# The input projection of a hybrid decoder layer by Strassen's scheme for pairs of token tiles, and a feed-forward pass in two groups

## What is computed

```python
hn = rmsnorm(x, norm1_g[l])
proj = hn @ w_in[l]                       # 1024 x 3608
q_a, k_a, v_a, gate_a, low_a, qkv_b, z_b, beta_b, dec_b = jnp.split(proj, IN_IDX, axis=-1)
...
o_a, h_a = gla_chunked(q, k, v, log_a.reshape(B, T, H_GLA, DK_GLA), st_gla[l])
...
o_b, h_b = gdn_chunked(qd, kd, vd, g, beta, st_gdn[l])
...
mix = jnp.concatenate([o_a.reshape(B, T, GLA_V), o_b.reshape(B, T, GDN_V)], axis=-1)
x = x + mix @ w_out[l]
hn2 = rmsnorm(x, norm2_g[l])
up, ffn_new = causal_dwconv(hn2 @ w_up[l], st_ffn[l], ffn_conv_w[l])
a_f, b_f = jnp.split(up, [D_FF], axis=-1)
x = x + (jax.nn.silu(a_f) * b_f) @ w_down[l]
```

## Time and profile before

| | us |
|---|---|
| median of 3 runs | 3298.98 |
| lowest and highest | 3298.91, 3301.03 |
| the profiled execution | 3301.26 |
| its span on the core | 3299.5 |
| TensorE busy in it | 3198.2 |
| VectorE | 2063.4 |
| ScalarE | 859.1 |
| GpSimd | 581.5 |

### The profile page before, as it was taken

One profiled execution on the slowest core, in us unless ns is written; L12 is line 12 of the kernel. 1 busy time (PEld: TensorE's weight loads), 2 busy tenths in 40 slices (PEclk: granted clock), 3 DMA queues, 4 the chain that ended last, 5 costly groups with the idle time before them and its releaser, 6 DMA issues.

```text
span 3299.5 us, 59597 instructions
## 1 busy us (share of the span) xinstructions
PE 3198.2 (97%) x23585; PEld 2178.1 (66%) x23585; DVE 2063.4 (63%) x4876; ACT 859.1 (26%) x1897; POOL 581.5 (18%) x945
## 2 busy tenths in 40 slices
PE   7999999999999999996799999999999999999999
PEld 3555555556555555554477777777768877888775
DVE  1566665655566665655566566666686666666668
ACT  1223333233223332232322111111232222222223
POOL 1111111111111111112231121111063112111110
PEclk9999999999999999997799999999999999999999
DMA  6022222222222212215531111111133111111112
GB/s 239 9 84 84 84 65 84 84 63 67 65 79 84 84 65 84 79 53 154 156 98 39 49 53 39 39 51 39 39 114 126 39 50 40 52 39 39 40 38 77
DMA packets 225314, 236.56 MB, mean 72 GB/s; under 512 B 14268, under 2 KB 169444, under 8 KB 225043
## 3 DMA queue, kind: packets, MB, share of 16 engines
q1 hardware_dynamic: 225043, 232.81, 22.4%
HBM read 203.10 MB, written 29.67 MB: 71 GB/s over the span
## 4 chain that ended last, share of the span: by engine, by line
PE 48%; DVE 1%; POOL 1%; ACT 0%; issue 0%; DVEq 0%; POOLq 0%
PE mlp_bank L2135 32%; PE mlp_bank L2209 15%; PE mlp_bank L2223 2%; DVE mcv L2577 0%; POOL acc L2457 0%; PE mlp_bank L2215 0%; POOL acc L2462 0%; DVE acc L2638 0%; ACT mcv L2298 0%; PE mlp_bank L2234 0%; PE mlp_bank L2221 0%; DVE raw L2521 0%; ACT mth L2312 0%; DVE mcv L2581 0%; ACT raw L2353 0%
## 5 line engine op out<-in xcount | busy, mean ns | idle before, releaser
L696 PE MATMUL mixer_bank<-arena,hnt 128*128 128x451 f32 x2048 | 868.0, 555 | 15.5 <-DMA arena<-in_w_in_dram 8.4
L2135 PE MATMUL mlp_bank<-arena,ws 128*128 128x176 f32 (+1 forms) x3520 | 657.6, 340 | 10.6 <-ACT raw L2325 9.0
L2135 PEld LDWEIGHTS mlp_bank<-arena,ws 128*128 128x128 f32 x3520 | 588.8, 190 | 49.0 <-ACT raw L2325 10.2
L696 PEld LDWEIGHTS mixer_bank<-arena,hnt 128*128 128x128 f32 x2048 | 367.4, 191 | 307.6 <-issue 302.6
L2209 PE MATMUL mlp_bank<-arena 128*128 128x512 f32 x1120 | 493.7, 592 | 0.0
L2610 DVE TENSOR_TENSOR acc<-acc,mlp_bank 128x512 f32<-128x512 f32 x560 | 370.5, 686 | 57.0 <-PE mlp_bank L2209 54.5
L2209 PEld LDWEIGHTS mlp_bank<-arena 128*128 128x128 f32 x1120 | 211.2, 190 | 231.7 <-issue 205.3
L2577 DVE SCALAR_TENSOR_TENSOR mcv<-raw,cf,mcv 128x512 f32<-128x512 f32 (+2 forms) x440 | 287.3, 670 | 68.5 <-ACT mcv L2298 58.2
L646 POOL TENSOR_TENSOR ex<-dtt,level 128x512 f32<-128x512 f32 (+1 forms) x114 | 142.9, 1253 | 939.8 <-DVE dtt L1645 641.6
L2135 PE MATMUL mlp_bank<-arena 128*128 128x176 f32 (+1 forms) x1320 | 254.9, 343 | 5.2 <-PEq L2720 4.3
L730 PE MATMUL mixer_bank<-wo,th 128*128 128x512 f32 x512 | 249.0, 609 | 3.0 <-DMA wo<-in_w_out_dram 2.4
(11 more groups left out here) (368 smaller groups left out, 3619.3 us busy)
## 6 DMA issues: line engine op xcount, KB each, us to landing
wo<-in_w_out_dram SPq DMA_DIRECT2D x260, 256.0 KB, 2.7
arena<-in_w_up_dram SPq DMA_DIRECT2D x44, 512.0 KB, 4.9
wu<-in_w_up_dram SPq DMA_DIRECT2D x44, 512.0 KB, 4.9
arena<-in_w_down_dram SPq DMA_DIRECT2D x40, 512.0 KB, 4.1
arena<-in_w_in_dram SPq DMA_DIRECT2D x7, 1804.0 KB, 16.2
...
```

Of the source, the lines that this page charges most:

```text
L696: x = pe.matmul(bank[ring(g)][0:N, 0:GW], hnt[:, k, 0:N], w[:, k, g * GW:(g + 1) * GW], start=(k == 0), stop=(k == KT - 1))
L2135: x = pe.matmul(out[:, 0:N], left[:, k, :], xb[:, slot, k, g * N:(g + 1) * N], start=first and k == 0, stop=k == HK - 1, skip_group_check= ...
```

## The change

**The projection.** Tiles 0 and 1 are both projected ahead of mixer 0, by 16 units (column group, tile) of eight matmuls in four banks. VectorE meanwhile forms sixteen sums T1 to T4 of weight halves (each 128x1804), in place of the arena's upper columns; SyncE stores them to DRAM (14.8 MB). The other fourteen tiles go in pairs: the mixers 2p and 2p+1 host the tiles 2p+2 and 2p+3. Each host computes seven products for each of two column groups, 14 products of four matmuls, 56 in place of 64. Their left operands (`xops`) are made once for a pair by eight GpSimd operations, `x_operands`; their right operands come partly from the arena and partly, ten chunks of 924 KB per host, through a ring of four buffers which SyncE fills. Eight products' results are copied out of their bank by ScalarE (`keep`), six are added to copies by VectorE (`make_c11`, `make_c12`, `make_c22`); SyncE stores the blocks to DRAM (12 per pair) and reloads `proj` whole (`load_proj`, 1.85 MB) ahead of each mixer.

**The slots.** The output projection stands in slots 0 to 4, 6, 8 and 10, the products in 28 others; 13, 19, 23 and 39 are empty. The banks of the y transposes change (7 in place of the projection's), and the second half of them waits for the copy of the first. ScalarE squares the tokens of a coming tile ahead of ked. The sample's projection is wholly in mixer 14, for which SyncE loads the upper half of w_in again (7.4 MB), and mixer 15 has none.

**Feed-forward.** The second pass takes two groups of 264 columns.

```diff
+HW = NIN // 2
+OUT_SLOTS = {0: 0, 1: 1, 2: 2, 3: 3, 4: 4, 6: 5, 8: 6, 10: 7}
+PRODUCT_SLOTS = {slot: p for p, slot in enumerate([5, 7, 9, 11, 12, 14, 15, 16, 17, 18, 20, 21, 22, 24] + list(range(25, 39)))}
...
+            def ring_chunk(n):
...
+                t, i = divmod(n, CHUNKS)
+                if n >= 4:
+                    before, k = divmod(n - 4, CHUNKS)
+                    sp.wait_ge(s_products, PRODUCTS * before + (k + 3 if k < 5 else k + 5))
...
+            def host(t):
...
+                load_proj(t + 1)
+                n = CHUNKS * t
+                even = t % 2 == 0
+                ring_chunk(n + 4)
+                if even:
...
+            sp.wait_ge(s_stage_stored, stored(HOSTS))
+            sp.wait_ge(s_products, PRODUCTS * HOSTS)
+            for g in range(4, GROUPS):
+                w_group(g)
             wo_chunks(t - 1, 20)
+            load_proj(t + 1)
...
+            def x_operands(p):
+
+                c, done = 2 * p + 2, 7 * p
...
+                if p:
+                    gp.wait_ge(s_products, PRODUCTS * 2 * p)
...
+                gp.tensor_tensor(a11, xc[:, 0:HK_IN, :], scale[0], ALU.mult).then_inc(s_xops_made, 1)
+                gp.tensor_tensor(hnt[:, 0:HK_IN, :], hnt[:, 0:HK_IN, :], scale[1], ALU.mult)
+                gp.tensor_tensor(a12, xc[:, HK_IN:KT, :], scale[0], ALU.mult).then_inc(s_xops_made, 1)
+                gp.tensor_tensor(a22, hnt[:, HK_IN:KT, :], scale[1], ALU.mult).then_inc(s_xops_made, 1)
+                gp.wait_ge(s_xops_made, done + 3)
+                gp.tensor_tensor(s1, hnt[:, 0:HK_IN, :], a22, ALU.add).then_inc(s_xops_made, 1)
+                gp.wait_ge(s_xops_made, done + 4)
+                gp.tensor_tensor(s2, s1, a11, ALU.subtract).then_inc(s_xops_made, 1)
+                gp.tensor_tensor(s3, a11, hnt[:, 0:HK_IN, :], ALU.subtract).then_inc(s_xops_made, 1)
+                gp.wait_ge(s_xops_made, done + 6)
+                gp.tensor_tensor(s4, a12, s2, ALU.subtract).then_inc(s_xops_made, 1)
+            x_operands(0)
             for t in range(1, TILES):
                 mixer(t, t + 1, False, True)
+                if t % 2 and t < HOSTS - 1:
+                    x_operands((t + 1) // 2)
...
+            def project_first(i, g, tile):
+
+                if i >= 4:
+                    pe.wait_ge(s_proj_out if FIRST[i - 4][1] == 0 else s_one_out,
+                               sum(e == FIRST[i - 4][1] for _, e in FIRST[:i - 3]))
+                if i < 2:
...
+                    x = pe.matmul(bank[(0, 1, 3, 4)[i % 4]][:, 0:GW], first_x[tile][:, k, :], weight(k, g),
                                   start=(k == 0), stop=(k == KT - 1))
...
+            def product(t, part):
+
+                q, half = divmod(part, 2)
+                pair = 7 * (t // 2)
+                j = column_group(t, q // 7)
+                run, add = bank[1], bank[0]
...
+                    n = CHUNKS * t + (q - 2 if q < 7 else q - 4)
+                    if half == 0:
+                        pe.wait_ge(s_ring_loaded[n % 4], 16 + 16 * (n // 4 + 1))
+                    right = wx[n % 4]
+                    left, out, first = {2: (S2_X, run, False), 3: (S1_X, add, True), 4: (S3_X, run, False),
+                                        5: (S4_X, add, False), 6: (A22, run, False), 9: (S1_X, add, True),
+                                        10: (S2_X, run, False), 11: (S4_X, add, False), 12: (S3_X, run, False),
+                                        13: (A22, run, False)}[q]
+                for k in range(2 * half, 2 * half + 2):
+                    x = pe.matmul(out[:, 0:GW], xops[:, left, k, :], right[:, k, :], start=first and k == 0,
+                                  stop=k == HK_IN - 1, skip_group_check=not first)
+                if half == 1:
+                    x.then_inc(s_products, 1)
...
+                    for slot in range(i, j):
+                        if slot in OUT_SLOTS:
+                            if t:
+                                project_out(t, OUT_SLOTS[slot], C, lambda: None)
+                        elif slot in PRODUCT_SLOTS:
+                            part = PRODUCT_SLOTS[slot]
+                            if t < HOSTS:
+                                product(t, part)
+                            elif t == HOSTS and part < KT:
+                                project_sample(0, part)
+                            elif t == HOSTS and part >= 12 and part % 2 == 0:
+                                project_sample(1, part // 2 - 6)
                 return fill
...
             def turn_y(t):
                 def turn(half):
 
-                    if t < TILES - 1:
-                        pe.wait_ge(s_proj_out, GROUPS * (t + 1) + 3 + half)
-                        y_turn(t, C, half)
-                    elif half == 1:
-                        pe.wait_ge(s_proj_out, GROUPS * (t + 1) + 8)
-                        y_turn(t, C, 0)
-                        y_turn(t, C, 1)
+                    if half == 0:
+                        pe.wait_ge(s_sg_new, t + 1)
+                    else:
+                        pe.wait_ge(s_hs_half, t)
+                    y_turn(t, C, half)
...
+            def keep(t, q, block, source):
+
+                act.wait_ge(s_products, PRODUCTS * t + q + 1)
...
+                    act.wait_ge(s_stage_stored, stored(t))
...
                     y_square(t, C)
+                    act.wait_ge(s_y_normed, 3 * t - 2)
+                front(0)
 
                 act.wait_ge(s_q_turned, n)
                 act.activation(qsq[0:N, :, :], heads(3)[0:N, :, :], ACT.Square).then_inc(s_q_squared, 1)
...
+            def add_product(t, q, out, block, bank_):
+
+                dve.wait_ge(s_products, PRODUCTS * t + q + 1)
+                v = stage[4 * (q // 7) + block]
+                if out is None:
+                    out = v
+                return dve.tensor_tensor(out, v, bank_[:, 0:GW], ALU.add)
+
...
+                    if a == 1 and hosts:
+                        make_c12(t, 0)
                     if a == 1 and out and not sample:
-                        if not last_prompt:
-                            keep_y_half(t, C, 0)
+                        keep_y_half(t, C, 0)
                     if a == NL - 1:
...
-        PASSES = ((0, 2, 256, 0, 8), (T // 2, 3, 176, 8, 9))
+        PASSES = ((0, 2, 256, 0, 8), (T // 2, 2, 264, 8, 9))
```

791 lines of the change are left out of this document (517 added, 274 removed).

## The result

| | median us | lowest, highest | runs |
|---|---|---|---|
| before | 3298.94 | 3297.58, 3301.03 | 4 |
| changed | 3433.94 | 3428.73, 3443.64 | 4 |

The ratio is 1.041, with a 95% interval of 1.0398 to 1.0423: 135 us slower, where +71 and at most 3410 were forecast. The profiled execution of the changed kernel took 3443.64 us (span 3441.9), the slowest of the four.

What follows compares the result with a forecast made beforehand. The prediction took chains over VectorE and ScalarE, not TensorE, to bound the mixers. Its terms, 38.9 + 4.4 + 27 + 5 + 1 + 9.4 - 9.6 - 1 - 4, summed to +71: 3370 us, range 3315 to 3410.

Steps and rivals of the forecast that it cites:

- TensorE is the bound: Rival: whatever matmul time TensorE is spared comes off, about 3250 us; chance 0.08.
- Term 1: Ahead of mixer 0: projecting tiles 0 and 1 up front starts mixer 0 at 109.5 instead of 70.64, +38.9 us.
- Term 2: Steady hosts 1 to 13: with four slots left empty, a mixer goes from 92.6 to 93.0 us, +4.4 together.
- Term 4: Clock: new waits, twice a mixer, may halve TensorE's granted clock; 0 to +44 us in 26 waits, taken as +5.
- rival with both costs near their upper bounds: GpSimd blocks VectorE for whole operations or the clock falls at each wait: 3390 to 3410 us; chance 0.18.
- Term 3: Head of mixers 2, 4, ... 12: GpSimd's operand operations delay ug and lengthen VectorE's; 4.5 us each, +27, between 0 and +50.
- Term 5: Other mixers: mixer 0 +1, mixer 14 +9.4 (waiting for w_out), mixer 15 -9.6, the sample's own mixer -1 us.
- Term 6: Feed-forward, second pass: two groups of 264 columns give -3 and fewer stalls -1, together -4 us.
- The starved queue: Rival: SyncE's one queue starves TensorE in every mixer, 5 us per host, 3435 us; chance 0.07.

Runs made afterwards that it cites:

- move_four: Changed kernel with product parts in other slots: 19, 23 and 39 filled, 13, 25, 36 and 37 empty; 3392.6 us.
- cover_39: Changed kernel with two unread 128x451 matmuls added in empty slot 39 of mixers 0 to 13; 3412.9 us.
- move_slots: Changed kernel with the same product parts in other slots: 19 and 39 filled, 25 and 36 empty in their place; 3386.7 us.
- ffn_only: Kernel before with only the feed-forward's second pass changed to two groups of 264 columns; 3294.7 us against 3301.3, ratio 0.9980.
- narrow_ops: move_slots with the eight GpSimd operand operations of mixers 2, 4, ... 12 cut to 2 of 128 columns; 3354.0 us.

## Why the prediction was right and wrong

**The bound: right.** Chains, not TensorE, limit a mixer. Taking 6.1 us of matmuls out of it gave no time back: mixer 5's 98.2 us less the 5.1 of the clock is 93.1, for 93.0 forecast, and the waits stand where the forecast put them, within 0.1 us. The rival "TensorE is the bound" is out, with every host at 94.9 us or more. The chain can be shorter than 93.0, though: emptying slots 25 and 36, where TensorE showed no hole, did give time, and move_four has odd mixers of 91.7 and 91.9 us at full clock throughout. The change left its empty slots where VectorE and ScalarE held TensorE anyway.

**Term 1: right.** +39.7 for +38.9.

**Term 2: right in an odd mixer's chain.** From L1196 to L1114 and on to L1135 the forecast was 41.4; measured 44.8, of which 3.4 are the first half-clock stretch. From the first L1207 to slot 24 it was 4.34 (3.84 before, and 0.5), measured 4.31.

**Term 4: this is the step that failed most.** It allowed 0 to 1.7 us for each of 26 waits, 44 at most, and took 5 for all, because "Around them TensorE is full". Measured: 63 us in mixers 1 to 13. Three things in it were wrong. Being full on both sides did not help. The upper bound was no bound: about 1.7 is what the one stretch in mixer 0 cost, and at the turn seven of the ten stretches were twice as long and cost 3.4 each. And 13 of the 28 stretches lay at waits that the term did not count, the two short ones of slot 23 and the one for gg. The experiments agree: covering the turn's wait took 22 us off mixers 1 to 13 (cover_39), and other slots for the same work 52 (move_slots). The prediction had the row that warned of it, a drop behind 1.76 us, and both waits it forecast were longer; it set the row aside with a reason for which it had no row. Its rival with both costs near their upper bounds, at 0.18, had the causes right, and even its 3410 was 24 us short. That a single row would have been a poor rule too is shown by ffn_only, where the same wait was followed by full clock.

**Term 3: right in kind and nearly in size, but without the clock.** It said 4.5 for an even mixer. Where it can be seen by itself (move_slots, narrow_ops) an even mixer is 7.2 longer, 3.8 by the chain and 3.4 by the clock behind the wait. In the changed kernel, take 63 for the clock and 4.4 for term 2 from the 86.2 of mixers 1 to 13, and 19 remain, 3.1 for each of the six; this split is an estimate, since stretches at half clock can lie over waits. The path was another than forecast: the term asked when ug comes, but TensorE waited for gg, behind VectorE's taps. Here the rule of the Trainium skill ("SBUF — State Buffer", "SBUF: two separate sides") describes what the rows show, one engine blocked for whole operations of the other: twelve taps took 4.3 us more beside GpSimd operations of 1.3, and the longest single tap, 1.31, is one such operation long. The 8.3 for an even mixer that the prediction tied to it was too dear, since it took GpSimd operations of 2.25 us, and they took 1.3.

**Term 5: mixer 0 failed, mixer 14 held, mixer 15 half.** "+1" had no row behind it, and 18.1 came. The forecast named VectorE's sums and their stores in term 1 as running beside TensorE, and asked only whether the ring would be ready; it didn't follow what stood behind them in VectorE's and SyncE's queues, the first decays of mixer 0. In mixer 14 the wait was 13.7 for 16 forecast. Mixer 15, from L1196 to L1196, gave 4.7 of its 9.6: ked was still waited for, 3.04 us instead of 4.04, a stretch of 4.06 us stands later for which the profile names no releaser, and 55 us of the mixer ran at half clock, after 41 before, where full clock had been assumed.

**Term 6: right in direction, too small.** -6.2 for -4, outside the 3 to 5 it gave itself, and 6.5 by itself. Its -3 does not follow closely from the figures beside it: 25.0 against 24.9 in 22 steps is 2.

**The starved queue: did not come.** The longest wait for w_out in the hosts was 0.3 us, at 190 GB/s.

What stays open: why the clock falls behind a given wait in one mixer or one execution and not in the next, as behind the 1.9 at the turn (10 of 13), the one for ked (5 of 13) and the pair at slot 23 (9 of 13). The experiments show that shorter waits there lower it less often; they give no length from which on it is certain or safe. Open too is why TensorE stood 0.89 and 1.24 us longer at L1207 in mixers 7 and 9.
